# Turning the feed-forward's inner values by DMA, as two 16-bit planes, instead of on TensorE

## The chip, the core and the metric

The kernel runs on one core of one Trainium2 chip. The metric is the device time of one execution in microseconds (us). The engines of a core work side by side, each through its own list of instructions in order: TensorE (PE, matmuls, with its weight loads shown apart as PEld), VectorE (DVE), ScalarE (ACT), GpSimd (POOL) and SyncE (SP, which here only issues DMAs). They wait for one another through semaphores. DMAs that any of them issues run on the core's 16 DMA engines.

## The reference

Two transformer blocks on 256 tokens of width 1024. What is computed between the four feed-forwards (attention of several kinds, gating, pooling) is not touched by the change. A feed-forward is

```
def swiglu(x, w_gate, w_up, w_down):
    return (jax.nn.silu(x @ w_gate) * (x @ w_up)) @ w_down

h = h + FFN_RES * swiglu(rms_norm(h, ffn1_norm[l]), ffn1_w_gate[l], ffn1_w_up[l], ffn1_w_down[l])
```

with 2816 inner values per token. It stands four times in the program: twice in the first block, once in each layer of the second. All is in 32-bit floats.

## The kernel before

**Weights.** All weights stream through SBUF in 404 units of 128 x 1024 values (512 KB). SP loads a unit with two DMAs of 256 KB into one of three buffers `raw`, as soon as VectorE is done with what was there (`free_raw`, line 411, which waits for `low_done`). ScalarE rounds the unit to its high part `wh` (`split`, line 661, the copy at line 659), VectorE takes the difference to get the low part `wl` (`split`, line 1173, the subtraction at line 1182) and then counts up `low_done`. There are six pairs `wh`/`wl`, so both engines may be up to six units ahead of TensorE, which counts up `units_used` when it is done with one. A product in full precision is three matmuls: high by high, high by low, low by high (`products`, lines 1799 to 1801). A unit is 12 matmuls of 512 columns.

**A feed-forward** (`ffn`, once in each engine's program; `f` is 0 to 3) cuts the 2816 inner values into 11 chunks of 256. In the names of TensorE's code, `gate_up(c)` is four units and computes gate and up of chunk c+1 into banks 0 and 1; `down_unit(c, 0)` and `down_unit(c, 1)` multiply chunk c by the down weights. Between them ScalarE computes silu of the gate half (line 721), VectorE multiplies with up (`mul_step`, line 1245) and so writes the inner values `hid`, which lie in the tensor `scores`, with tokens on the partitions. The down product needs them turned. In the kernel before TensorE does that with four 128 x 128 transposes against an identity (`transpose_hidden`, line 1893) into bank 6; ScalarE copies bank 6 rounded to `hTh` (`ht_step`, line 727), VectorE writes `hTl`, the difference (line 1251). `ht_high` and `ht_low` count the two.

**Order around it.** TensorE's loop over c from 1 to 8 is `gate_up(c)`, a wait for `ht_low`, the two down units of c, the transposes of c+1. So the transposes of a chunk run right after the down units of the chunk before, and their result is wanted only after four further units. ScalarE's loop `body` is four splits, silu, two splits, `ht_step`. VectorE's is the same with `mul_step` in the place of silu. Both engines split four units ahead (`LEAD`): while TensorE begins the down units of a chunk, the splits right behind silu are those of the third and fourth unit of the next `gate_up`. Counted from a silu as number 0, with the unit u+8 as the first of the two down units then running, the two splits behind silu are units u+12 and u+13, and the next four are u+14 to u+17. The next `gate_up` is units u+10 to u+13, the down units behind it u+14 and u+15.

**Loads of other kinds.** GpSimd issues bulk loads of its own, of constants and of the second input, while feed-forwards 0 and 1 run.

Of the kernel before, what the change touches and what calls it, by code (L numbers as in the profile page):

```python
# [22 lines left out]
F32 = mybir.dt.float32  # L23
F32R = mybir.dt.float32r
I32 = mybir.dt.int32
ACT = mybir.ActivationFunctionType
AX = mybir.AxisListType

P = 128
T = 256  # L30
NT = T // P
# [3 lines left out]
FC = 256  # L35
NFC = FF // FC
# [92 lines left out]
def two_block_kernel(nc, d, out):  # L129
    ctx = ExitStack()  # L130
    with ctx:
# [3 lines left out]
        def sem(name):  # L135
            return ctx.enter_context(nc.semaphore(name))
# [75 lines left out]
        hid = scores[:, :, 0:FC]  # L212

# [62 lines left out]
        ht_low = sem("ht_low")  # L276
        acc_done = sem("acc_done")
# [371 lines left out]
        def _(act):  # L649
# [66 lines left out]
            def ffn(f, tail=None):  # L716
# [7 lines left out]
                def ht_step(c, dst):  # L724

                    act.wait_ge(ht_psum, NFC * f + c + 1)
                    copy(dst, bank[6][:, :]).then_inc(ht_high, 1)

                def body(c, dst):
                    for i in range(4):  # L730
                        split(u + 4 + i, c)

                    act.wait_ge(units_used, u + 8 + 6 * c)
                    silu_step(c + 1)
                    for i in range(2):
                        split(u + 8 + i, c)
                    ht_step(c + 1, dst)
# [16 lines left out]
                ht_step(0, hTh[:, :, :])  # L754
                with act.Fori(0, NFC - 2, 1) as c:
                    body(c, hTh[:, :, :])

                body(NFC - 2, aTh[:, 6:8, :])
# [402 lines left out]
        def _(dve):  # L1161
# [76 lines left out]
            def ffn(f, done, norm_after, tail=None):  # L1238
# [14 lines left out]
                def body(c, low, high):  # L1253
                    for i in range(4):
                        split(u + 4 + i, c)
                    mul_step(c + 1)
                    for i in range(2):
                        split(u + 8 + i, c)
                    ht_step(c + 1, low, high)
# [5 lines left out]
                with dve.Fori(0, NFC - 2, 1) as c:  # L1265
                    body(c, hTl[:, :, :], hTh[:, :, :])

                body(NFC - 2, aTl[:, 6:8, :], aTh[:, 6:8, :])
# [524 lines left out]
        def _(pe):  # L1793
# [90 lines left out]
            def ffn(f, norm_after, middle=None, late=None):  # L1884
# [40 lines left out]
                transpose_hidden(1)  # L1925
                with pe.Fori(1, NFC - 2, 1) as c:
                    gate_up(c)

                    pe.wait_ge(ht_low, NFC * f + 1 + c)
                    for k in range(2):  # L1930
                        down_unit(c, k)
                    transpose_hidden(c + 1)

                c = NFC - 2
                gate_up(c)
# [553 lines left out]
```

## Time and profile before

| | us |
|---|---|
| median of 3 runs | 1237.26 |
| the runs | 1236.86 to 1239.22 |
| the profiled execution | 1238.18 |
| its span, first to last instruction | 1236.0 |
| TensorE busy | 1226.8 |
| VectorE busy | 750.8 |
| ScalarE busy | 646.2 |

The profiled execution lies 0.9 us over the median, and 2.2 us of it lie around the span. Busy time of TensorE counts the matmuls' modelled durations, which overlap; how fast it goes is read from the distance between the starts of its matmuls. The granted clock of TensorE is 1.000 over the whole span. "Idle" behind a row of a timeline is the time in which the engine stood before that instruction, and what ended it.

### The profile page before, as it was taken

The page shows a single profiled execution, that of the slowest core. Times are in us where ns is not written, and L with a number is a line of the kernel's source. Part 1 is how long each engine was busy: PE and PEld are TensorE (multiplying, and loading weights), DVE is VectorE, ACT ScalarE, POOL GpSimd, SP SyncE. Part 2 cuts the span into 40 slices and gives each one's busy share as a digit, 9 for nine tenths or more (in the row PEclk, how much of TensorE's full clock was granted, in tenths as well). Part 3 has the DMA queues.
Part 4 walks back from the last instruction along what each step waited for, and adds up shares of the span by engine and source line. Part 5 has one row for each costly group of instructions (what it writes and reads, how often), then busy time and mean ns, then how long its engine had stood idle before and what let it go on. Part 6 is the DMA issues. An engine that isn't in the chain of part 4 may idle for free.

```text
span 1236.0 us, 17479 instructions
## 1 busy us (share of the span) xinstructions
PE 1226.8 (99%) x5862; PEld 1009.8 (82%) x5862; DVE 750.8 (61%) x1017; ACT 646.2 (52%) x939; POOL 67.7 (5%) x122
## 2 busy tenths in 40 slices
PE   8999999999999999999999999999999999999998
PEld 7888888877788888888888788888888887888887
DVE  5554546697775564547768666654556666655544
ACT  6454445575555454446666566544445456643442
POOL 0540000000000000000220110000000000000000
PEclk9999999999999999999999999999999999999999
DMA  7876564544555776564555416756565553665662
GB/s 221 238 233 188 186 204 137 179 145 154 161 162 155 247 220 191 184 203 139 177 162 187 154 60 182 231 177 196 181 199 161 163 164 92 199 209 184 189 198 91
DMA packets 166737, 219.43 MB, mean 178 GB/s; under 512 B 13680, under 2 KB 108640, under 8 KB 166560
## 3 DMA queue, kind: packets, MB, share of 16 engines
q1 hardware_dynamic: 164608, 213.70, 55.4%
q0 software_dynamic: 1648, 4.75, 1.3%
q8 instruction: 30, 0.49, 0.2%
q10 hardware_dynamic: 432, 0.33, 0.1%
q14 instruction: 19, 0.16, 0.0%
HBM read 217.68 MB, written 1.05 MB: 177 GB/s over the span
## 4 chain that ended last, share of the span: by engine, by line
PE 96%; ACT 1%; DVE 1%; DMA 1%; issue 0%; SPq 0%; POOL 0%; ACTq 0%; DVEq 0%; POOLq 0%
PE bank L1799 29%; PE bank L1801 29%; PE bank L1800 29%; PE bank L1855 2%; PE bank L1893 2%; PE bank L2051 1%; PE bank L2038 1%; PE bank L2067 1%; PE bank L2036 0%; ACT sb_wh L659 0%; ACT sb_probs L1101 0%; DMA sb_raw<-w_up 0%; PE bank L1972 0%; DVE sb_wl L1182 0%; PE bank L2388 0%
## 5 line engine op out<-in xcount | busy, mean ns | idle before, releaser
L1182 DVE TENSOR_TENSOR sb_wl<-sb_raw,sb_wh 128x1024 fp32r<-128x1024 f32 x403 | 485.2, 1223 | 219.5 <-ACT sb_wh L659 214.6
L659 ACT ACTIVATE sb_wh<-sb_raw 128x1024 fp32r<-128x1024 f32 (+1 forms) x405 | 419.5, 1055 | 231.4 <-DMA sb_raw<-ffn_w_up 74.7
L1799 PE MATMUL bank<-sb_wh,sb_aTh 128*128 128x512 f32 (+1 forms) x1132 | 443.6, 392 | 1.2 <-DVE sb_wl L1182 0.7
L1801 PE MATMUL bank<-sb_wh,sb_aTl 128*128 128x512 f32 (+1 forms) x1132 | 434.9, 384 | 0.0
L1800 PE MATMUL bank<-sb_wl,sb_aTh 128*128 128x512 f32 (+1 forms) x1132 | 434.1, 384 | 0.0
L1801 PEld LDWEIGHTS bank<-sb_wh,sb_aTl 128*128 128x128 f32 x1132 | 212.7, 188 | 43.2
L1799 PEld LDWEIGHTS bank<-sb_wh,sb_aTh 128*128 128x128 f32 x1132 | 212.8, 188 | 42.3 <-issue 2.0
L1800 PEld LDWEIGHTS bank<-sb_wl,sb_aTh 128*128 128x128 f32 x1132 | 213.1, 188 | 39.2
L1799 PE MATMUL bank<-sb_wh,sb_hTh 128*128 128x512 f32 x320 | 124.9, 390 | 0.0
L1801 PE MATMUL bank<-sb_wh,sb_hTl 128*128 128x512 f32 x320 | 124.7, 390 | 0.0
L1800 PE MATMUL bank<-sb_wl,sb_hTh 128*128 128x512 f32 x320 | 124.5, 389 | 0.0
L721 ACT ACTIVATE sb_junk<-bank,sb_rstd 128x256 f32<-128x256 f32 x88 | 36.9, 470 | 100.9 <-PE bank L1801 100.9
L1245 DVE SCALAR_TENSOR_TENSOR sb_scores<-bank,sb_rstd,sb_junk 128x256 f32<-128x256 f32 x88 | 38.5, 479 | 74.3 <-ACT sb_junk L721 74.3
L1799 PE MATMUL bank<-sb_wh,sb_yTh 128*128 128x512 f32 x192 | 77.6, 404 | 0.0
L1801 PE MATMUL bank<-sb_wh,sb_yTl 128*128 128x512 f32 x192 | 75.0, 391 | 0.0
L1800 PE MATMUL bank<-sb_wl,sb_yTh 128*128 128x512 f32 x192 | 74.9, 390 | 0.0
L659 ACT ACTIVATE sb_hTh<-bank 128x512 fp32r<-128x512 f32 x40 | 23.8, 595 | 96.3 <-PE bank L1893 96.3
L1251 DVE TENSOR_TENSOR sb_hTl<-bank,sb_hTh 128x512 fp32r<-128x512 f32 x40 | 27.6, 691 | 70.6 <-ACT sb_hTh L659 70.5
L1801 PEld LDWEIGHTS bank<-sb_wh,sb_hTl 128*128 128x128 f32 x320 | 60.1, 188 | 12.5
L1800 PEld LDWEIGHTS bank<-sb_wl,sb_hTh 128*128 128x128 f32 x320 | 60.1, 188 | 12.4
L1799 PEld LDWEIGHTS bank<-sb_wh,sb_hTh 128*128 128x128 f32 x320 | 60.1, 188 | 12.3
L659 ACT ACTIVATE sb_aTh<-bank,sb_vecs 128x256 fp32r<-128x256 f32 x72 | 28.3, 475 | 38.7 <-PE bank L1855 38.7
(235 smaller groups left out, 835.7 us busy)
## 6 DMA issues: line engine op xcount, KB each, us to landing
sb_raw<-ffn_w_down SPq DMA_DIRECT2D x88, 256.0 KB, 3.0
sb_raw<-w_gate SPq DMA_DIRECT2D x88, 256.0 KB, 3.4
sb_raw<-w_up SPq DMA_DIRECT2D x88, 256.0 KB, 4.1
sb_raw<-w_down SPq DMA_DIRECT2D x88, 256.0 KB, 2.9
sb_raw<-ffn_w_gate SPq DMA_DIRECT2D x87, 256.0 KB, 3.4
sb_raw<-ffn_w_up SPq DMA_DIRECT2D x87, 256.0 KB, 4.2
sb_raw<-w_in SPq DMA_DIRECT2D x80, 256.0 KB, 3.0
sb_raw<-e_w_in SPq DMA_DIRECT2D x40, 256.0 KB, 3.0
```

Source lines behind the costliest of these rows:

```text
L659: return act.activation(dst, src, ACT.Copy, scale=scale)
L721: act.activation(silu[:, t, :], bank[first_bank + t][:, 0:FC], ACT.Silu, scale=rs(norm, t))\
L1182: dve.tensor_tensor(wl[:, u % NSPLIT, :], raw[:, u % NRAW, :], wh[:, u % NSPLIT, :].bitcast(F32), ALU.subtract).then_inc(low_done, 1)
L1245: dve.scalar_tensor_tensor(hid[:, t, :], bank[first_bank + t][:, FC:2 * FC], rs(norm, t), silu[:, t, :], ALU.mult, ALU.mult).then_inc(h_re ...
L1251: dve.tensor_tensor(low, bank[6][:, :], high.bitcast(F32), ALU.subtract).then_inc(ht_low, 1)
L1799: pe.matmul(dst, lh, w_hi, start=start, stop=False)
L1800: pe.matmul(dst, lh, w_lo, start=False, stop=False)
L1801: return pe.matmul(dst, ll, w_hi, start=False, stop=stop)
L1855: ins = pe.transpose(dst[:, T * j + P * t:T * j + P * t + P], tiles(j, t), ident[:])
L1893: ins = pe.transpose(bank[6][:, T * j + P * t:T * j + P * t + P], hid[:, t, tok(j)], ident[:])
L2038: pe.matmul(bank[4 + i % 2][:, P:3 * P], q[:, P:T], k[:, 0:T], start=True, stop=True).then_inc(at.s_psum, 1)
L2051: ins = pe.transpose(bank[6][:, tok(j)], probs[:, i % 4, tok(j)], ident[:])
```

## The change

The inner values of chunks 1 to 9 of each feed-forward are turned by a DMA. Chunks 0 and 10 keep TensorE's transposes. A DMA transpose takes 16-bit elements, so the 32-bit values are split into a plane of the lower and a plane of the upper halves, turned as bits, and joined again.

- ScalarE, behind silu and one split, waits for `mul_step` (`h_ready`), copies the lower and the upper halves of `hid` into `planes` (two copies of 128 x 512 values of 16 bits, read at a step of two), does the next split, whose instruction also waits for `planes_done`, and issues one DMA transpose of `planes` into `planesT` (256 KB, eight blocks of 128 x 128).
- VectorE, in the next pass of the loop and behind three of its four splits, waits for the DMA (`planes_turned`) and joins the halves in `hT` with two copies of 128 x 512 (`join_step`). After the fourth split it waits for `ht_high` and writes `hTl` (`turned_step`), and only then comes to `mul_step`.
- ScalarE, behind its four splits and ahead of silu, waits for `hT_joined` and copies `hT`, rounded, to `hTh`.
- TensorE loses the transposes of chunks 1 to 9, 36 groups of four in the program. In their place it waits for `h_ready` ahead of `gate_up`, since `gate_up` overwrites the banks from which `mul_step` reads.

```
 [ScalarE]
-                def ht_step(c, dst):
+                def ht_step(n, dst):

-                    act.wait_ge(ht_psum, NFC * f + c + 1)
+                    act.wait_ge(ht_psum, 2 * f + n)
                     copy(dst, bank[6][:, :]).then_inc(ht_high, 1)

-                def body(c, dst):
+                def planes_step(c):
+
+                    act.wait_ge(h_ready, 2 * NFC * f + 2 + 2 * c)
+                    for h in range(2):
+                        ins = copy(planes.rearrange("p (h t c) -> p h t c", h=2, t=NT)[:, h], hid_halves[:, h])
+                    ins.then_inc(planes_done, 1)
+
+                def turned_step(c):
+
+                    act.wait_ge(hT_joined, (NFC - 2) * f + c)
+                    copy(hTh[:, :, :], hT).then_inc(ht_high, 1)
+
+                def turn_hidden():
+                    act.dma_start_transpose(planesT.rearrange("p (b r) -> p b r", r=P), planes).then_inc(planes_turned, 16)
+
+                def body(c, turned, tail_chunk=False):
                     for i in range(4):
                         split(u + 4 + i, c)
+                    if turned:
+                        turned_step(c)

                     act.wait_ge(units_used, u + 8 + 6 * c)
                     silu_step(c + 1)
-                    for i in range(2):
-                        split(u + 8 + i, c)
-                    ht_step(c + 1, dst)
+                    split(u + 8, c)
+                    if tail_chunk:
+                        split(u + 9, c)
+                        return
+                    planes_step(c + 1)
+
+                    act.wait_ge(planes_done, (NFC - 2) * f + 1 + c)
+                    split(u + 9, c)
+                    turn_hidden()
 [VectorE]
+                def join_step(c):
+
+                    dve.wait_ge(planes_turned, 16 * (NFC - 2) * f + 16 * c)
+                    turned = planesT.rearrange("p (h t k r) -> p h k t r", h=2, t=NT, k=2)
+                    for h in range(2):
+                        ins = dve.tensor_copy(hT_halves[:, h], turned[:, h])
+                    ins.then_inc(hT_joined, 1)
+
+                def turned_step(c):
+
+                    dve.wait_ge(ht_high, NFC * f + c + 1)
+                    dve.tensor_tensor(hTl[:, :, :], hT, hTh[:, :, :].bitcast(F32), ALU.subtract).then_inc(ht_low, 1)
+
-                def body(c, low, high):
-                    for i in range(4):
+                def body(c, turned):
+                    for i in range(3):
                         split(u + 4 + i, c)
+                    if turned:
+                        join_step(c)
+                    split(u + 7, c)
+                    if turned:
+                        turned_step(c)
                     mul_step(c + 1)
                     for i in range(2):
                         split(u + 8 + i, c)
-                    ht_step(c + 1, low, high)
 [TensorE]
-                transpose_hidden(1)
                 with pe.Fori(1, NFC - 2, 1) as c:
+
+                    pe.wait_ge(h_ready, 2 * NFC * f + 2 + 2 * c)
                     gate_up(c)

                     pe.wait_ge(ht_low, NFC * f + 1 + c)
                     for k in range(2):
                         down_unit(c, k)
-                    transpose_hidden(c + 1)
```

The lists of instructions show what moved. ScalarE's loop, from silu to the loop's end, before (`sb_junk` holds silu):

```order
L721 ACTIVATE sb_junk<-bank,sb_rstd 128x256 [waits units_used]
L721 ACTIVATE sb_junk<-bank,sb_rstd 128x256
L669 REGISTER_ALU
L672 REGISTER_ALU [waits loaded0]
L659 ACTIVATE sb_wh<-sb_raw 128x1024 [waits units_used]
L659 ACTIVATE sb_wh<-sb_raw 128x1024 [waits units_used,loaded1]
L726 REGISTER_ALU
L659 ACTIVATE sb_hTh<-bank 128x512 [waits ht_psum]
L755 REGISTER_ALU
L755 COMPARE_AND_BRANCH
```

and in the changed kernel, from the copy to `hTh` on (`sb_probs` holds both planes and turned planes, `sb_probsT` is `hT`):

```order
L668 ACTIVATE sb_hTh<-sb_probsT 128x512 [waits hT_joined]
L759 REGISTER_ALU
L730 ACTIVATE sb_junk<-bank,sb_rstd 128x256 [waits units_used]
L730 ACTIVATE sb_junk<-bank,sb_rstd 128x256
L678 REGISTER_ALU
L681 REGISTER_ALU [waits loaded0]
L668 ACTIVATE sb_wh<-sb_raw 128x1024 [waits units_used]
L740 ISA
L668 ACTIVATE sb_probs<-sb_scores 128x512 [waits h_ready]
L668 ACTIVATE sb_probs<-sb_scores 128x512
L668 ACTIVATE sb_wh<-sb_raw 128x1024 [waits units_used,loaded1,planes_done]
L751 DMA_TRANSPOSE sb_probs<-sb_probs 128x8x128
```

The copy to `hTh` went from behind the second split to a place ahead of silu, and two copies stand between the two splits, with the DMA behind them. VectorE's loop, from the third of its four splits on, before:

```order
L1182 TENSOR_TENSOR sb_wl<-sb_raw,sb_wh 128x1024 [waits high_done]
L1181 REGISTER_ALU
L1182 TENSOR_TENSOR sb_wl<-sb_raw,sb_wh 128x1024 [waits high_done]
L1244 ISA
L1245 SCALAR_TENSOR_TENSOR sb_scores<-bank,sb_rstd,sb_junk 128x256 [waits silu_done]
```

and in the changed kernel:

```order
L1216 TENSOR_TENSOR sb_wl<-sb_raw,sb_wh 128x1024 [waits high_done]
L1289 REGISTER_ALU
L1292 COPY sb_probsT<-sb_probs 128x512 [waits planes_turned]
L1292 COPY sb_probsT<-sb_probs 128x512
L1215 REGISTER_ALU
L1216 TENSOR_TENSOR sb_wl<-sb_raw,sb_wh 128x1024 [waits high_done]
L1297 REGISTER_ALU
L1298 TENSOR_TENSOR sb_hTl<-sb_probsT,sb_hTh 128x512 [waits ht_high]
L1278 ISA
L1279 SCALAR_TENSOR_TENSOR sb_scores<-bank,sb_rstd,sb_junk 128x256 [waits silu_done]
```

The two copies that join and the subtraction to `hTl` now stand around the fourth split, behind the third, where the subtraction came before only after two further splits.

## Rows read from the trace of the kernel before

**Rows 1.** The page: engines' busy time, and the chain that ended last.

```profile
PE 1226.8 (99%) x5862; PEld 1009.8 (82%) x5862; DVE 750.8 (61%) x1017; ACT 646.2 (52%) x939; POOL 67.7 (5%) x122
PE 96%; ACT 1%; DVE 1%; DMA 1%; issue 0%; SPq 0%; POOL 0%; ACTq 0%; DVEq 0%; POOLq 0%
```

**Rows 2.** TensorE's waits, the largest in total: us in total, times, longest.

```profile
PE bank L2377 <- DVE sb_probs L1708: 2.1, 4, 0.8
```

**Rows 3.** Timeline of TensorE, one chunk: start us, us, instruction.

```profile
105.38 0.39 PE L1801 MATMUL bank<-sb_wh,sb_hTl 128*128 128x512 f32 x1
105.61 0.60 PE L1893 MATMUL bank<-sb_ident,sb_scores 128*128 128x128 f32 x4
...
108.12 0.39 PE L1799 MATMUL bank<-sb_wh,sb_aTh 128*128 128x512 f32 x1
...
116.96 0.39 PE L1799 MATMUL bank<-sb_wh,sb_hTh 128*128 128x512 f32 x1
```

**Rows 4.** Timeline of ScalarE, same chunk; "x2" are two instructions.

```profile
100.36 0.84 ACT L721 ACTIVATE sb_junk<-bank,sb_rstd 128x256 f32<-128x256 f32 x2 [3.36 <-PE bank L1801]
101.09 2.01 ACT L659 ACTIVATE sb_wh<-sb_raw 128x1024 fp32r<-128x1024 f32 x2
...
106.73 2.00 ACT L659 ACTIVATE sb_wh<-sb_raw 128x1024 fp32r<-128x1024 f32 x2
110.01 1.06 ACT L659 ACTIVATE sb_wh<-sb_raw 128x1024 fp32r<-128x1024 f32 x1 [1.27 <-DMA sb_raw<-ffn_w_up]
```

**Rows 5.** Timeline of VectorE, same chunk.

```profile
102.18 2.36 DVE L1182 TENSOR_TENSOR sb_wl<-sb_raw,sb_wh 128x1024 fp32r<-128x1024 f32 x2 [0.44 <-ACT sb_wh L659]
...
111.10 1.23 DVE L1182 TENSOR_TENSOR sb_wl<-sb_raw,sb_wh 128x1024 fp32r<-128x1024 f32 x1 [0.92 <-ACT sb_wh L659]
113.90 1.22 DVE L1182 TENSOR_TENSOR sb_wl<-sb_raw,sb_wh 128x1024 fp32r<-128x1024 f32 x1 [1.58 <-ACT sb_wh L659]
```

**Rows 6.** Timeline of SP, same chunk: the load of unit u+16 begins.

```profile
104.98 0.38 SPq L440 DMA_DIRECT2D sb_raw<-ffn_w_gate  x1
```

**Rows 7.** Groups by line: busy us, mean ns of one.

```profile
L659 ACT ACTIVATE sb_wh<-sb_raw 128x512 fp32r<-128x512 f32 x2 | 1.1, 628 | 0.0
L1708 DVE TENSOR_SCALAR sb_probs<-sb_probs,sb_rinv 128x256 f32<-128x256 f32 x16 | 4.9, 351 | 0.3
L1492 DVE COPY sb_gates<-bank 128x512 f32<-128x512 f32 x2 | 1.4, 687 | 2.3 <-PE bank L1855 2.3
L1251 DVE TENSOR_TENSOR sb_hTl<-bank,sb_hTh 128x512 fp32r<-128x512 f32 x40 | 27.6, 691 | 70.6 <-ACT sb_hTh L659 70.5
```

**Rows 8.** The page: DMA queue (packets, MB, share), and an issue's us to landing.

```profile
q1 hardware_dynamic: 164608, 213.70, 55.4%
sb_raw<-ffn_w_up SPq DMA_DIRECT2D x87, 256.0 KB, 4.2
```

**Rows 9.** Stretches: us, each engine's busy time, clock, DMA share, GB/s.

```profile
62.00:64.00 2.00, 2.00 (x10) 1.66 (x9) 0.00 (x0) 0.00 (x0) 1.44 (x7) 1.00 1.06 349
102.50:104.50 2.00, 2.00 (x11) 1.65 (x10) 2.00 (x2) 0.60 (x1) 0.00 (x0) 1.00 0.00 0
```

**Rows 10.** Timelines in feed-forwards 0 and 1: VectorE, ScalarE and TensorE beside GpSimd's bulk loads.

```profile
64.75 1.06 ACT L659 ACTIVATE sb_wh<-sb_raw 128x1024 fp32r<-128x1024 f32 x1 [7.38 <-DMA sb_raw<-ffn_w_down]
66.56 0.39 PE L1799 MATMUL bank<-sb_wh,sb_hTh 128*128 128x512 f32 x1
436.70 0.39 PE L1799 MATMUL bank<-sb_wh,sb_hTh 128*128 128x512 f32 x1
437.57 2.54 DVE L1182 TENSOR_TENSOR sb_wl<-sb_raw,sb_wh 128x1024 fp32r<-128x1024 f32 x2 [2.00 <-ACT sb_wh L659]
```

**Rows 11.** Timelines at feed-forward 2's first pass: ScalarE, VectorE, TensorE.

```profile
775.62 0.82 ACT L721 ACTIVATE sb_junk<-bank,sb_rstd 128x256 f32<-128x256 f32 x2
787.46 1.23 DVE L1182 TENSOR_TENSOR sb_wl<-sb_raw,sb_wh 128x1024 fp32r<-128x1024 f32 x1 [1.50 <-ACT sb_wh L659]
790.16 0.39 PE L1799 MATMUL bank<-sb_wh,sb_hTh 128*128 128x512 f32 x1
```

More of the change, by code:

```diff
@@ L25 @@
 I32 = mybir.dt.int32
+U16 = mybir.dt.uint16
 ACT = mybir.ActivationFunctionType
@@ L212, in two_block_kernel @@
         hid = scores[:, :, 0:FC]
+        hid_halves = scores[:, :, :].bitcast(U16).rearrange("p t (c h) -> p h t c", h=2)[:, :, :, 0:FC]
+        planes = probs[:, 2, :].bitcast(U16)
+        planesT = probs[:, 3, :].bitcast(U16)
+        hT = probsT[:, 0, :].rearrange("p (k t) -> p k t", k=2)
+        hT_halves = probsT[:, 0, :].bitcast(U16).rearrange("p (k t r h) -> p h k t r", k=2, t=NT, h=2)
         soft = shared[:, 0:768].rearrange("p (s c) -> p s c", s=2)
@@ L276, in two_block_kernel @@
         ht_low = sem("ht_low")
+        planes_done = sem("planes_done")
+        planes_turned = sem("planes_turned")
+        hT_joined = sem("hT_joined")
         acc_done = sem("acc_done")
@@ L753, in ffn @@
                 splits(u + 2, 2)
[L754 to L758, printed above, removed]
+                ht_step(1, hTh[:, :, :])
+                body(0, False)
+                with act.Fori(1, NFC - 2, 1) as c:
+                    body(c, True)
+                body(NFC - 2, True, True)
+                ht_step(2, aTh[:, 6:8, :])
                 if tail is not None:
@@ L1264, in ffn @@
                 ht_step(0, hTl[:, :, :], hTh[:, :, :])
-                with dve.Fori(0, NFC - 2, 1) as c:
-                    body(c, hTl[:, :, :], hTh[:, :, :])
-                body(NFC - 2, aTl[:, 6:8, :], aTh[:, 6:8, :])
+                body(0, False)
+                with dve.Fori(1, NFC - 2, 1) as c:
+                    body(c, True)
+                body(NFC - 2, True)
+                ht_step(NFC - 1, aTl[:, 6:8, :], aTh[:, 6:8, :])
                 if tail is not None:
@@ L1931, in ffn @@
                         down_unit(c, k)
-                    transpose_hidden(c + 1)
                 c = NFC - 2
+                pe.wait_ge(h_ready, 2 * NFC * f + 2 + 2 * c)
                 gate_up(c)
```

## The prediction

> **What bounds the kernel now.** I read the page first. TensorE is busy for 99% of the span and the chain that ended last is TensorE for 96% of it [rows 1]. The list of waits confirms it: the wait that costs TensorE most in the whole program sums to 2.1 us [rows 2]. So the time is the number of matmuls by their distance, and two things alone move it: work taken from TensorE, and a wait of TensorE that was not there. Busy times of ScalarE and VectorE (52% and 61%) say that there is room on average. Whether there is room at the right moment is what the timelines are for. In a steady chunk ScalarE stands idle for 3.36 us ahead of silu, until TensorE ends the four gate and up units [rows 4]; the splits behind silu are therefore tied to TensorE's pace, and their loads after them.
>
> **What the change removes.** The matmul ahead of the four transposes starts at 105.38 and the tenth behind them at 108.12, 2.74 us [rows 3]. From there the next down unit, 39 matmuls on, starts at 116.96: 8.84 / 39 = 0.2267 us each. Ten steps would be 2.27 us, so a group of transposes costs 0.47 us. 36 groups go: 36 x 0.47 = 16.9 us, all on the path, since TensorE never waits there. ScalarE's and VectorE's old steps for the turned values (0.69 us on VectorE [rows 7]) are replaced by others of the same kind.
>
> **What it adds, in a steady chunk.** The new chain is: silu, product, two plane copies, DMA, join, copy to hTh, subtraction to hTl; it must end before the next down unit. What matters is not its own length but what it queues behind and what queues behind it.
>
> (a) Plane copies. 128 x 512 from SBUF on ScalarE took 0.63 us [rows 7]; two of them, with the overlap of 0.1 us that two splits in a row show (2.01 us for 2 x 1.06) [rows 4], are 1.05 us. They stand ahead of the split of unit u+13. VectorE was done with that unit at 102.18 + 2.36 = 104.54 [rows 5], and is now at 105.6. The load of u+16, which needs this buffer, began at 104.98 [rows 6], and begins 0.6 us later.
>
> (b) The DMA. No row shows a transpose. Its 0.26 MB at the rate that the weight queue shows while it is busy, 213.7 MB / (0.554 x 1236 us) = 312 GB/s [rows 8], take 0.85 us of all DMA engines. If it is cut into 1,024 rows of 128 values, each as dear as that queue's mean packet, 0.554 x 16 x 1236 / 164,608 = 67 ns [rows 8], it takes 1,024 x 67 / 16 = 4.3 us. I take 1.1 us, near the lower end, since these rows carry a fifth of that mean packet's bytes. The DMA engines have idle stretches (0 GB/s from 102.5 to 104.5 us [rows 9]), but not there: it is issued at about 103.1 + 1.05 = 104.2, when u+15 and u+16 are being loaded. Of 0.6 us of (a) and 1.1 us of (b) I put 0.7 us on the arrival of u+16, because a load that begins later stands less long behind that of u+15. So VectorE ends u+16 at 111.10 + 1.23 + 0.7 = 113.0 [rows 5]. The planes themselves, landed after 4.2 us like a weight load of that size [rows 8], are there at 108.4, 4.6 us early. How long ScalarE is held by the issue is not shown either. SP's 0.38 us [rows 6] is the nearest row; ScalarE's next splits, u+14 and u+15, began at 106.73 before [rows 4], so an issue of up to 2.5 us from 104.2 on delays nothing.
>
> (c) The join. It stands behind the split of u+16. A copy of 128 x 512 took 0.69 us from PSUM, an operation of 128 x 256 within SBUF 0.35 us [rows 7]; the copies lie between 0.35 and 0.69. I take 0.45, so 0.9 us for both: 113.9.
>
> (d) The split of u+17 on VectorE, 1.15 us, and the subtraction, 0.69 us less 0.1 of overlap [rows 5, 7]: 115.7. ScalarE's copy to hTh (0.63 us) runs beside the split.
>
> (e) The deadline is the next down unit: 116.96 - 0.47 = 116.5. The chain is 0.8 us early. At the low ends (nothing for the DMA, 0.35 us a copy) it is 1.7 us early. At the high ends (4.3 us and 0.69 us) it is nearly 4 us late. What hid the old chain was 9 us of air between the transposes and their use; now there is under one.
>
> How lateness is paid: silu waits for the gate and up units, not for the down units that stall. So if the chain is x late, the next chunk's chain starts as early as ever and its deadline lies x later. A chain that is y late in every chunk then costs y/2 a chunk.
>
> **Where the deadline is missed in any case.** In a feed-forward's first pass the splits run behind. In feed-forward 2 silu starts at 775.62, though TensorE had ended the units before it one chunk (72 x 0.2267 + 0.47 = 16.8 us) ahead of 790.16, at 773.4 [rows 11]. VectorE ends u+16 at 787.46 + 1.23 = 788.7. With the same 0.7 + 0.9 + 1.15 + 0.6 = 3.35 us the chain ends at 792.0; the deadline is 790.16 - 0.47 = 789.7: 2.3 us of stall. Feed-forwards 1 and 3 read alike, 0 is just in time: 3 x 2.3 = 6.9 us.
>
> GpSimd's bulk loads collide twice with the stream. From 62 to 64 us the DMA engines are full at 349 GB/s [rows 9], ScalarE waits 7.38 us and splits u+16 only from 64.75 [rows 10]. TensorE did not notice, since it had split units in store. Now the join stands behind that split: 64.75 + 1.06 + 1.23 + 3.35 = 70.4 against a deadline of 66.56 - 2 x 0.47 = 65.6: 4.8 us. In feed-forward 1: 437.57 + 1.23 + 3.35 = 442.15 against 436.70 - 0.94 + 2.3 (the stall before it) = 438.1 [rows 10]: 4.1 us. Together 8.9 us.
>
> The clock: every row shows a granted clock of 1.00, full speed, and TensorE's longest wait among those costliest is 0.8 us [rows 2, 9]. The Trainium skill (TensorE: Matmul & The Clock Gate, Rules for kernel authors) warns that idle gaps between bursts of matmuls of the length of the largest stalls here can take the clock to its lower level. No row here shows that, and the sum holds nothing for it; it would add to the slower side.
>
> **Sum.** -16.9 + 6.9 + 8.9 = -1.1 us. The profiled execution's 1238.18 becomes 1237.1; that execution lies 0.9 us over the median, so I forecast **1236 us**. A measurement of this kernel can tell about 0.2% (2.5 us) from no change, so this is no change: the work saved is given back as five stalls.
>
> **Rivals.**
>
> *The chain is cheap.* The stream has air, so the DMA delays nothing, the copies take 0.35 us (0.9 us less in the chain), and the first passes catch up because the old steps no longer stand among their splits. Then only the collisions remain, 4.8 + 4.1 less 0.9 each and with the stall of 2.3 gone from the second one's deadline: 3.9 + 5.5 = 9.4, at most; at the least, if the second collision's chain also catches up, 7. Net some -8.5 us: 1229. For it: the DMA engines' share of 0.55. Against: they are full just where it counts.
>
> *Late in every chunk: slower.* The transpose's packets cost DMA time above (b), u+16 comes later, the join with it. It decides from 0.8 us above my sum; at 1.8 us above, the chain is 1 us late, 31 chunks by 0.5 us and 5 stalls by 1 us: +20 us, 1257. For it: the interval of (b) reaches 3.2 us above my value. Against: the rate at which wide packets move, and idle stretches ahead of the loads.
>
> *The transpose itself is long.* It may take 8.8 us before the join waits for it (113.0 - 104.2). If its eight blocks go one after another and it lands after 12.6 us, three times a load's 4.2, the chain ends at 104.2 + 12.6 + 0.9 + 1.15 + 0.6 = 119.5, 3 us late: 31 x 1.5 = 46 us more in the chunks and up to 3 us at each of the five stalls, some 1290. Against it: a load of the same size lands after 4.2 us [rows 8]. The Trainium skill (VectorE: DVE Perf Modes, The three transpose paths) gives 1309 ns for one 128 x 128 block by DMA; eight in a row would be 10.5 us, an estimate from that page, which the trace of before can neither confirm nor deny, and by which the chain would be 0.9 us late.
>
> **Chances.** Forecast case 0.42 (1231 to 1243), cheap chain 0.20, late in every chunk 0.31, long transpose 0.07. Faster by over 0.2% (under 1234.8): 0.20 and four tenths of the first, 0.37. Slower (over 1239.7): 0.29 + 0.07 and a seventh of the first, 0.42. Within: 0.21. Range 1226 to 1262: it reaches from a little below the cheap chain's time to a little above that of the late chain, and leaves out the long transpose and the edges.
>
> **What would show it.** Distance of TensorE's starts at the end of a down unit back to 0.2267 us with no 1893 group: the gain. In TensorE's waits, VectorE's subtraction to hTl as releaser: about five waits, of 2 to 5 us, at the first passes of feed-forwards 1 to 3 and near 66 and 438 us. About 35 such waits: the late chain. VectorE's join waiting for the DMA and not for the split ahead: the long transpose. Plane copies other than 0.6 us, join copies other than 0.45 us, and u+16 later by other than 0.7 us would correct a term each. The forecast is wrong if the first passes or the collisions do not stall TensorE, or if the steady chunks do.

## The result, and the profile after

The changed kernel took **1244.35 us** (median of 7 runs, 1240.77 to 1249.9) against 1237.32 for the kernel before beside it (7 runs, 1236.86 to 1239.22): ratio **1.0055**, 95% interval 1.0045 to 1.0064. It is 7 us slower; the forecast was 1236 us, no change. The profiled execution took 1245.88 us, with a span of 1244.1, 8.1 us longer than before. The runs spread more than those of before, 9 us against 2.4.

The page of the changed kernel: the DMA queue that carries the transposes (packets, MB, share of 16 engines), and the chain that ended last.

```profile
q10 hardware_dynamic: 38448, 9.77, 4.6%
PE 81%; DMA 7%; DVE 4%; ACT 4%; issue 2%; SPq 1%; ACTq 0%; POOL 0%; DVEq 0%; POOLq 0%
```

TensorE's share of the chain fell from 96% [rows 1] to 81%: DMA, VectorE and ScalarE now stand in it, a sign of stalls. It is no measure of them: 15% of the span are 187 us, and the stalls are 19, since behind each stall the chain is followed back over the other engines for much longer than TensorE stood. TensorE's waits, the two largest (us in total, times, longest):

```profile
PE bank L1852 <- DVE sb_hTl L1298: 17.9, 6, 4.8
PE bank L2432 <- DVE sb_probs L1761: 2.1, 4, 0.8
```

The second row is what was the largest before [rows 2]. The first is new: six waits for VectorE's subtraction to hTl. By the starts of the matmuls around them, less a normal step of 0.227 us, their lengths are 2.55 and 4.99 us (feed-forward 0, at 49 and 68 us), 1.25 and 3.72 (feed-forward 1, at 424 and 442), 3.55 (feed-forward 2, at 797) and 2.87 (feed-forward 3, at 1094): 18.9 us in all. All are in chunk 1 or 2. The one in feed-forward 2, in TensorE's timeline:

```profile
797.24 0.39 PE L1854 MATMUL bank<-sb_wh,sb_aTl 128*128 128x512 f32 x1
801.02 0.79 PE L1852 MATMUL bank<-sb_wh,sb_hTh 128*128 128x512 f32 x1 [3.39 <-DVE sb_hTl L1298]
801.61 0.63 PE L1853 MATMUL bank<-sb_wl,sb_hTh 128*128 128x512 f32 x1
802.03 0.63 PE L1854 MATMUL bank<-sb_wh,sb_hTl 128*128 128x512 f32 x1
```

Behind the stall a matmul takes 0.63 us where it took 0.39 before it, and the starts lie 0.43 us apart, not 0.227. Stretches around the longest stall show why (stretch; us; busy time of TensorE, its weight loads, VectorE, ScalarE and GpSimd; granted clock; DMA share; GB/s):

```profile
68.00:70.00 2.00, 0.06 (x1) 0.00 (x0) 0.92 (x1) 1.60 (x2) 1.66 (x5) 1.00 0.52 145
70.00:72.00 2.00, 0.00 (x0) 0.00 (x0) 2.00 (x4) 1.44 (x4) 1.83 (x3) 0.55 0.55 167
72.89:76.30 3.41, 3.41 (x8) 2.76 (x9) 2.23 (x4) 2.69 (x4) 2.59 (x7) 0.50 0.67 230
80.00:84.00 4.00, 4.00 (x19) 3.31 (x18) 0.95 (x2) 1.42 (x2) 0.00 (x0) 1.00 1.02 282
```

The granted clock fell to 0.50, the lower of the two levels (1.2 GHz), while TensorE stood, and stayed there for the first 4 us of work. This came at four of the six stalls, those of 4.99, 3.72, 3.55 and 2.87 us; the half-speed stretches are 6.8 us (part of it inside the stall) and three times 3.4 us long. In the kernel before, the clock was at 1.00 throughout.

In the steady chunks TensorE does not wait, as forecast. One of them: VectorE from the split of u+15 on, ScalarE's copies and the issue of the DMA, and TensorE's first matmul of the down units:

```profile
116.76 1.23 DVE L1216 TENSOR_TENSOR sb_wl<-sb_raw,sb_wh 128x1024 fp32r<-128x1024 f32 x1 [2.05 <-ACT sb_wh L668]
118.48 1.23 DVE L1216 TENSOR_TENSOR sb_wl<-sb_raw,sb_wh 128x1024 fp32r<-128x1024 f32 x1 [0.50 <-ACT sb_wh L668]
119.62 0.80 DVE L1292 COPY sb_probsT<-sb_probs 128x512 uint16<-128x512 uint16 x2
121.22 1.23 DVE L1216 TENSOR_TENSOR sb_wl<-sb_raw,sb_wh 128x1024 fp32r<-128x1024 f32 x1 [0.80 <-ACT sb_wh L668]
122.36 0.69 DVE L1298 TENSOR_TENSOR sb_hTl<-sb_probsT,sb_hTh 128x512 fp32r<-128x512 f32 x1
...
109.46 1.14 ACT L668 ACTIVATE sb_probs<-sb_scores 128x512 uint16<-128x512 uint16 x2
...
110.64 1.25 ACTq L751 DMA_TRANSPOSE sb_probs<-sb_probs  x1
...
123.91 0.39 PE L1852 MATMUL bank<-sb_wh,sb_hTh 128*128 128x512 f32 x1
```

The chain ends at 123.05, 0.9 us ahead of the matmul that needs it (0.8 to 1.9 us in the 26 steady chunks of the trace, 1.3 at the median); the join waits for the split ahead of it and not for the DMA.

### The profile page after: what moved, and what is told of

It is laid out like the page before. It is cut to its first block, busy times and chain, and to the rows that moved or that the text cites. A ratio compares the mean times of both kernels' runs of the same rounds, so it can differ in the third digit from the quotient of the medians.

```text
span 1244.1 us, 17351 instructions
## 1 busy us (share of the span) xinstructions
PE 1216.9 (98%) x5718; PEld 999.6 (80%) x5718; DVE 776.9 (62%) x1089; ACT 692.0 (56%) x1011; POOL 66.6 (5%) x122
## 4 chain that ended last, share of the span: by engine, by line
PE 81%; DMA 7%; DVE 4%; ACT 4%; issue 2%; SPq 1%; ACTq 0%; POOL 0%; DVEq 0%; POOLq 0%
PE bank L1852 25%; PE bank L1854 25%; PE bank L1853 25%; DMA sb_raw<-ffn_w_up 4%; ACT sb_wh L668 2%; DVE sb_wl L1216 2%; PE bank L1908 2%; DMA sb_raw<-w_up 2%; PE bank L2106 1%; SPq L449 1%; PE bank L2093 1%; DMA sb_raw<-w_out 1%; PE bank L2122 1%; PE bank L2091 0%; ACT sb_probs L1135 0%
## 5 line engine op out<-in xcount | busy, mean ns | idle before, releaser
L668 ACT ACTIVATE sb_wh<-sb_raw 128x1024 fp32r<-128x1024 f32 (+1 forms) x405 | 425.6, 1057 | 283.0 <-DMA sb_raw<-ffn_w_down 50.5
L1852 PE MATMUL bank<-sb_wh,sb_hTh 128*128 128x512 f32 x320 | 128.5, 402 | 17.9 <-DVE sb_hTl L1298 17.9
L1853 PEld LDWEIGHTS bank<-sb_wl,sb_hTh 128*128 128x128 f32 x320 | 61.9, 193 | 12.9
L1229 DVE SCALAR_TENSOR_TENSOR sb_aTl<-bank,sb_vecs,sb_aTh 128x256 fp32r<-128x256 f32 x72 | 30.0, 477 | 25.5 <-ACT sb_aTh L668 25.3
L1854 PEld LDWEIGHTS bank<-sb_wh,sb_yTl 128*128 128x128 f32 x192 | 36.0, 188 | 7.8
```

The lines of the kernel that those rows point to most:

```text
L668: return act.activation(dst, src, ACT.Copy, scale=scale)
L1229: dve.scalar_tensor_tensor(aTl[:, k, :], bank[6 + g % 2][:, T * j:T * j + T], vecs[:, col + k:col + k + 1], aTh[:, k, :].bitcast(F32), ALU ...
L1852: pe.matmul(dst, lh, w_hi, start=start, stop=False)
L1853: pe.matmul(dst, lh, w_lo, start=False, stop=False)
L1854: return pe.matmul(dst, ll, w_hi, start=False, stop=stop)
```

## The experiments

All ratios are against the kernel before, run beside them (medians 1237.6 to 1237.9). A helper number: with no stall and the clock at 1.00, a feed-forward takes 155.5 us from the transposes of chunk 0 to those of chunk 10 (159.9 before), so the 36 groups are worth 4 x 4.36 = 17.4 us. The first rows below are the changed kernel's feed-forward 1, the last two the same place in the kernel with an early join and loads apart (below):

```profile
402.27 0.60 PE L1946 MATMUL bank<-sb_ident,sb_scores 128*128 128x128 f32 x4
564.51 0.60 PE L1946 MATMUL bank<-sb_ident,sb_scores 128*128 128x128 f32 x4
```

```profile
392.91 0.60 PE L1967 MATMUL bank<-sb_ident,sb_scores 128*128 128x128 f32 x4
548.43 0.60 PE L1967 MATMUL bank<-sb_ident,sb_scores 128*128 128x128 f32 x4
```

162.24 less 155.52 is 6.7 us, of which the two stalls are 4.97; the other 1.75 us are lost in the matmuls behind the stalls. The same in feed-forward 0 gives 9.75 - 7.54 = 2.2 us, in 2 and 3 together 9.74 - 6.42 = 3.3 us: 7.3 us in all. Not all of it is the clock's: behind the two stalls that left the clock at 1.00, 60 steps also took 0.14 us more than 60 x 0.2267. Six times 0.14 taken off, **6.4 us of clock** are left, 1.4 to 1.9 us for each of the four falls. The balance of the four feed-forwards is -17.4 + 18.9 + 7.3 = +8.8 us; the rest of the program was 0.7 us shorter, which gives the +8.1 of span.

### 1. The join earlier

```diff
 [ScalarE]
-for i in range(4): split(u + 4 + i, c)
-if turned: turned_step(c)
+for i in range(2): split(u + 4 + i, c)
+if turned: turned_step(c)
+for i in range(2, 4): split(u + 4 + i, c)
 [VectorE]
-for i in range(3): split(u + 4 + i, c)
-if turned: join_step(c)
-split(u + 7, c)
-if turned: turned_step(c)
+split(u + 4, c)
+if turned: join_step(c)
+split(u + 5, c)
+if turned: turned_step(c)
+for i in range(2, 4): split(u + 4 + i, c)
```

> The changed kernel with the chain taken forward: VectorE joins behind the first of its four splits (not the third) and subtracts behind the second; ScalarE copies to hTh behind its second split. Everything is still computed. Theory A (the stalls come from the join's place behind the split of unit u+16, and the clock's fall comes from the stalls): the join now stands behind u+14, which is split some 4 us earlier even where the stream is late, so the six waits of TensorE for hTl (18.9 us over a normal step in the changed kernel) go but for at most one or two, the granted clock stays at 1.00, and what is left is the gain of 36 groups of transposes, 16.9 us: about 1237.3 - 16.9 = 1220 us, 1219 to 1224. Rival B (the transpose lands late, or the added DMA traffic delays the stream itself): the join waits for the DMA, issued some 4 us before, or the splits come late anyway; four or more of the six stalls stay, and the time stays over 1236 us.

1227.28 us (5 runs, 1226.36 to 1230.96), ratio 0.9923, interval 0.991 to 0.9937. TensorE's wait for hTl:

```profile
PE bank L1855 <- DVE sb_hTl L1300: 4.0, 2, 3.4
```

Theory A in its mechanism, but 7 us over the 1220 us that it named and 3 over its band: four of six stalls went; those left are 0.7 and 3.6 us long, and the clock fell once. The larger one, at 66 us, has a new cause: the DMA transpose is itself late, and the join waits for it:

```profile
66.93 0.81 DVE L1294 COPY sb_probsT<-sb_probs 128x512 uint16<-128x512 uint16 x2 [1.69 <-DMA sb_probs<-sb_probs]
```

It stands behind a split of ScalarE that came at 60.03 us (54.25 in the changed kernel), beside GpSimd's loads, and landed 6.9 us after its issue, where the median is 4.4.

### 2. The join between the two places

The same edit with the join behind the second split, the subtraction and ScalarE's copy behind the third.

> The place between the two: join behind VectorE's second split (unit u+15), subtraction behind the third; ScalarE's copy to hTh behind its third. Theory (each stall shrinks by the time between VectorE's splits of u+15 and u+16 at its place in the changed kernel's trace: 1.5 of 2.55 us, 2.7 of 4.99, 1.7 of 1.25, 1.5 of 3.72, 3.6 of 3.55, about as much in feed-forward 3): three stalls stay, 1.1 + 2.3 + 2.2 us, with at most one fall of the clock: 1237.6 - 16.9 + 5.6 + 0 to 1.5 = 1226 to 1228 us. Rival (the stalls come from the DMA transpose's own landing or from a stream slowed everywhere, not from the order on VectorE): little difference from the changed kernel, 1240 us or more.

1232.23 us (4 runs), ratio 0.996, interval 0.9946 to 0.9975. The profiled execution took 1231.4 us:

```profile
PE bank L1854 <- DVE sb_hTl L1299: 8.6, 5, 5.0
```

Most of the effect is there and the order of the three places is as the theory has it (1244, 1232, 1227 us), but it is 4 us over the sum. Stall by stall the theory did less well. In feed-forward 0 the first was 1.2 us for 1.1 and the second, at 66 us, 5.2 for 2.3, with the one long fall of the clock behind it; in feed-forward 1 the second was 1.2 for 2.2; in feed-forward 2, where none was expected, 1.4.

### 3. Without the DMA

```diff
-                    turn_hidden()
...
-                    dve.wait_ge(planes_turned, 16 * (NFC - 2) * f + 16 * c)
-                    turned = planesT.rearrange(...)
+                    dve.wait_ge(planes_done, (NFC - 2) * f + c)
+                    turned = planes.rearrange(...)
```

> The changed kernel without its 36 DMA transposes: VectorE joins the planes as they lie, so the inner values of chunks 1 to 9 are not turned (this part of the computation is left out). ScalarE no longer spends its 1.25 us a chunk on the issue, and 9.4 MB less go through the DMA engines. Every copy, split and wait keeps its place. Theory A (place): the stalls stay, only shorter by what the DMA added to the arrival of unit u+16, 0.7 us each in the prediction: six stalls of some 2 to 4.5 us, about 1244.3 - 6 x 0.7 - 2 for a clock that falls less often = 1238 us. Rival B (the DMA or its issue makes the stalls): most of them go, and the time falls to 1220 to 1226 us.

1237.31 us (10 runs), ratio 0.9999, interval 0.999 to 1.0009.

```profile
PE bank L1851 <- DVE sb_hTl L1297: 12.0, 6, 3.4
```

All six stalls stay, 12.9 us in all instead of 18.9, with two falls of the clock instead of four. Five are 1.1 to 1.5 us shorter, the first of feed-forward 1 is 0.6 us longer (1.9 us). So the stalls are there without the DMA, as the theory of the place has it; the DMA and its issue add 1.0 us to each on average, by one trace of each kernel.

### 4. All that was added, nothing removed

TensorE keeps its transposes; plane copies, DMA transposes and joins are done beside them, into a tensor that nobody reads.

> The kernel before, with all that the change adds and nothing of what it removes: plane copies, the 36 DMA transposes issued from ScalarE at the same place, and VectorE's two join copies behind its third split, into a tensor that nobody reads. TensorE keeps its transposes, and what it waits for is the old chain. Theory A (what costs is only that TensorE's input now stands behind u+16): TensorE does not wait, and the time is that of before, 1237 us, within 2 us. Rival B (the added work or traffic itself pushes the splits beyond their deadlines): TensorE waits for wl or wh at the two collisions or in the first passes, and the time is 1241 us or more.

1239.73 us (10 runs, 1236.76 to 1245.79), ratio 1.002, interval 1.0006 to 1.0034: at the upper end of what theory A allows. The profiled execution, 1241.7 us, shows where the 2 us come from:

```profile
PE bank L1840 <- DVE sb_wl L1211: 2.9, 2, 2.1
```

TensorE waits at 69 us for a split: with the added work GpSimd's loads empty the store of split units, which they did not do before. This wait is 2.3 us long, the clock fell behind it, and the 60 matmuls behind it took 1.4 us more than normal: 3.7 of the 3.9 us of span over the kernel before. Elsewhere in this trace the added work is free.

### 5. TensorE turns chunks 1 and 2 too

```diff
-                with pe.Fori(1, NFC - 2, 1) as c:
+                for c in (1, 2):
+                    transpose_hidden(c)
+                    gate_up(c)
+                    pe.wait_ge(ht_low, NFC * f + 1 + c)
+                    for k in range(2):
+                        down_unit(c, k)
+                with pe.Fori(3, NFC - 2, 1) as c:
```

> The changed kernel with chunks 1 and 2 of each feed-forward turned by TensorE as before, and only chunks 3 to 9 by DMA. Eight groups of transposes come back, 8 x 0.47 = 3.8 us. Theory A: the six stalls are all in the first or second chunk turned by DMA while the stream of weights is behind; from chunk 3 on it has caught up. The stalls go, the clock stays at 1.00, and 28 x 0.47 = 13.2 us are gained: 1237.3 - 13.2 = 1224 us, 1222 to 1227. Rival B (whichever chunk is the first turned by DMA meets the stall, since the chain's own length makes it): four stalls stay at chunk 3, and the time is 1234 us or more.

1232.92 us (10 runs, 1226.74 to 1235.79), ratio 0.9959, interval 0.9945 to 0.9973. That is over theory A's band; the profiled execution, 1229.11 us, was one of two in which the clock stayed at 1.00. In feed-forwards 2 and 3 theory A held, no stall is left. In 0 and 1 chunk 3 stalls now (TensorE's timeline at 85 and 453 us):

```profile
85.05 0.49 PE L1874 MATMUL bank<-sb_wh,sb_hTh 128*128 128x512 f32 x1 [2.60 <-DVE sb_hTl L1310]
453.52 0.49 PE L1874 MATMUL bank<-sb_wh,sb_hTh 128*128 128x512 f32 x1 [2.41 <-DVE sb_hTl L1310]
```

These are 2.76 and 2.57 us by the starts. They could have been read from the trace of the kernel before: there VectorE ended u+16 of chunk 3 only 0.8 us (at 82.05) and 1.8 us (at 451.25) ahead of the deadline of (e), where a steady chunk has 4 to 5 us. The stream needs longer than one chunk to recover from GpSimd's loads.

### 6. GpSimd's loads apart

GpSimd's bulk loads of these two feed-forwards in pieces of at most 256 KB, one or two of them behind each wait for `units_used` from the 30th unit of the feed-forward on; one of them as example:

```diff
-pool.dma_start(gates[:, 0, :], bass.AP(bg.tensor, bg.offset, [[0, P], [1, 2 * D]])).then_inc(bias_in, 16)
+for i in range(4):
+    pool.wait_ge(units_used, 30 + 3 * i)
+    w = 2 * D // 4
+    pool.dma_start(gates[:, 0, i * w:(i + 1) * w], bass.AP(bg.tensor, bg.offset + i * w, [[0, P], [1, w]])).then_inc(bias_in, 16)
```

> The changed kernel with GpSimd's bulk loads of feed-forwards 0 and 1 cut in pieces of at most 384 KB and issued later, one each three to six units, instead of all at once near 53 to 57 us and 425 to 430 us. The chain keeps its place. Theory A (two of the six stalls, those of 4.99 and 3.72 us, come from these loads that push back the weight stream): both go, with the two stretches at half speed behind them that came after 73 and 446 us (6.8 and 3.4 us long, some 4.5 us of loss), and the other four stay: 1244.3 - 8.7 - 4.5 = 1231 us, 1229 to 1235. Rival B (the second chunk is late because it follows the first pass, whatever GpSimd loads): both stalls stay, 1242 us or more.

1236.3 us (10 runs, 1233.04 to 1238.97), ratio 0.999, interval 0.998 to 0.9999.

```profile
PE bank L1870 <- DVE sb_hTl L1316: 9.6, 5, 2.9
```

The stalls at 68 and 442 us are gone, as theory A has it: these two came from the loads. One of 1.5 us came at 517 us, behind a later piece, the clock fell behind those at 49 and 787 us (for 3.4 and 6.8 us), and the time is 1 us over the expected band.

### 7. The stalls filled

```diff
+FILL = ((7, 16), (0, 12), (11, 0), (9, 0))
...
+                    for _ in range(FILL[f][c - 1]):
+                        pe.matmul(bank[6][:, :], aTh[:, 0, tok(0)], aTh[:, 0:2, :], start=True, stop=True)
                     pe.wait_ge(ht_low, NFC * f + 1 + c)
```

> The changed kernel with filler for TensorE ahead of its wait for hTl: matmuls of 128x512 on values that lie there anyway, into bank 6, which nobody reads at that time; 7 and 16 of them in chunks 1 and 2 of feed-forward 0, 12 in chunk 2 of feed-forward 1, 11 and 9 in chunk 1 of feed-forwards 2 and 3, each set about 1 us shorter than the stall it fills (stalls of 2.55, 4.99, 3.72, 3.55 and 2.87 us, a matmul 0.227 us). The input of the down units comes as late as before, so nothing of the stalls is gained; but TensorE never stands for long. Theory A (what is left unexplained, about 6 us, is the clock's fall after the stalls): the granted clock stays at 1.00, no stretch of 3.4 us at half speed, and the time falls by 5 to 7 us to 1237 to 1239 us. Rival B (the clock falls for another reason, or its cost is not these 6 us): 1244 us or more, since filler never shortens the chain.

Median 1248.37 us (6 runs, 1238.95 to 1257.13), ratio 1.0108, interval 1.0083 to 1.0132. The profiled execution was the 1238.95 one: clock at 1.00 throughout, and 7 us less than the changed kernel's, as theory A has it. The input was about as late as there, 18.2 us over the six places for 18.9. The other five had clocks of 0.992 to 0.997 and no trace, and the median lies 4 us above the changed kernel's, where rival B would put it. A second trace of the same kernel:

> The same kernel as the one with filled stalls, for a second trace: its profiled execution had a granted clock of 1.00 and 1239.0 us, but its others had 0.992 to 0.997 and up to 1257 us. Reading A (the stream's timing differs from one execution to the next, and a stall longer than its filler plus 2.5 us lets the clock fall all the same, and a filler then runs at half speed in the next chunk): this trace, if it is a slow one, shows stalls behind the fillers of over 2.5 us or stalls where no filler stands, each with a stretch at 0.5. Reading B (the filler itself takes the clock down): stretches at 0.5 that begin inside or right behind fillers with no stall ahead of them.

1250.86 us in its profiled execution, 1253.16 median of 2. TensorE at feed-forward 0, chunk 2, where the filler ends and the wait begins:

```profile
68.14 3.79 PE L1984 MATMUL bank<-sb_aTh 128*128 128x512 f32 x16
77.58 0.79 PE L1853 MATMUL bank<-sb_wh,sb_hTh 128*128 128x512 f32 x1 [5.65 <-DVE sb_hTl L1299]
```

Here the input was 4.4 us later than in the changed kernel's trace, and TensorE stood for 5.65 us behind the filler; in feed-forward 1, chunk 1, which had no filler, for 4.54 us. The clock fell at both, and no fall came inside or behind a filler without a stall. Reading A. Why the input is later in most executions of this kernel is not shown. The trace also shows that the size of the stalls differs from one execution to the next: ScalarE got unit u+15 at 65.30 us in the changed kernel's trace and at 70.14 here, behind the same loads.

### 8. Pauses of known length

```diff
 [GpSimd]
+for c in range(1, 9):
+    pool.wait_ge(units_used, FIRST["ffn3"] + 8 + 6 * c)
+    pool.memset(qkT[...][:, 0:PAUSE[c - 1]], 0.0).then_inc(pause_over, 1)
 [TensorE]
                     gate_up(c)
+                    if f == 3:
+                        pe.wait_ge(pause_over, c)
                     pe.wait_ge(ht_low, NFC * f + 1 + c)
```

> The kernel before, with eight pauses of TensorE of rising length in feed-forward 3, one in each of chunks 1 to 8, 17 us or more apart: ahead of its wait for hTl TensorE waits for GpSimd to clear 1100, 1600, 2100, 2400, 2700, 3000, 3500 and 4096 values per partition, about 1 ns each. It measures the disputed price by itself. Theory A (a stall of about 3 us or more takes the granted clock to 0.5 for 3.4 us after it, which costs half of that, 1.7 us; shorter stalls cost their own length): the pauses of 1.1 to 2.4 us leave the clock at 1.00, those from about 2.8 us on do not; three or four falls: pauses of 20.5 us and some 0.3 us of overhead each, 23 us, plus 5 to 7 us: 1237.5 + 29 = 1266 us. Rival B (the clock falls for another reason, such as the DMA traffic or the changed kernel's own work): no falls, 1260 us. Rival C (any stall over 1 us can do it): falls after the short ones too, 1270 us or more.

1267.07 us (4 runs), 1263.0 in the profiled one, span 1260.8. The pauses by the starts of the matmuls were 1.29, 1.71, 2.12, 2.37, 2.62, 2.87, 3.29 and 3.79 us, 20.1 in all. TensorE behind the fourth, the fifth and the seventh, and stretches behind these and the eighth:

```profile
1144.62 0.40 PE L1806 MATMUL bank<-sb_wl,sb_hTh 128*128 128x512 f32 x1
...
1163.83 0.50 PE L1805 MATMUL bank<-sb_wh,sb_hTh 128*128 128x512 f32 x1 [2.46 <-POOL sb_qkT L649]
1164.17 0.56 PE L1806 MATMUL bank<-sb_wl,sb_hTh 128*128 128x512 f32 x1
1164.53 0.63 PE L1807 MATMUL bank<-sb_wh,sb_hTl 128*128 128x512 f32 x1
...
1206.84 0.50 PE L1805 MATMUL bank<-sb_wh,sb_hTh 128*128 128x512 f32 x1 [3.13 <-POOL sb_qkT L649]
1207.17 0.40 PE L1806 MATMUL bank<-sb_wl,sb_hTh 128*128 128x512 f32 x1
```

```profile
1145.70:1149.00 3.30, 3.30 (x17) 2.71 (x16) 0.58 (x1) 0.00 (x0) 0.00 (x0) 1.00 0.66 206
1164.40:1167.40 3.00, 3.00 (x8) 2.33 (x8) 1.18 (x2) 0.00 (x0) 0.00 (x0) 0.50 0.50 177
1208.00:1211.00 3.00, 3.00 (x15) 2.47 (x14) 0.00 (x0) 0.00 (x0) 0.00 (x0) 1.00 0.77 254
1229.10:1231.90 2.80, 2.80 (x8) 2.23 (x7) 0.00 (x0) 0.00 (x0) 0.00 (x0) 0.50 0.84 281
```

Theory A, but without the bound that it put near 2.8 us: the clock fell after 2.62, 2.87 and 3.79 us and did not after 3.29. In the other traces it fell after stalls of 2.0 us (loads apart, at 51 us) and 2.3 us (all added, at 69 us), and not after 2.56, 2.75 (chunks 1 and 2 on TensorE) and 2.91 us (loads apart). Each of the seven stalls over 3.3 us in the traces without filler was followed by a fall. The price: from one group of transposes to the next (16.80 us without a pause) the five chunks without a fall are longer than their pause by 0.14 to 0.16 us, the three with one by 1.75, 1.49 and 1.75: **1.3 to 1.6 us a fall** of 3.4 us at half speed. In the other traces falls of that length cost 1.3 to 1.6 us too, and those of 6.8 us 1.9 to 2.9. GpSimd's clearing stands for any stall here: no DMA transpose runs in this kernel, so the falls belong to the standing, not to the change's own work. The other three runs had clocks of 0.992 instead of 0.996, about twice the time at half speed, and 4 to 5 us more.

### 9. Early join and loads apart

> Both together: the join behind the first split, as in the run with the early join (1227.3 us, with stalls of 0.7 and 3.6 us left, both in feed-forward 0, the larger at the bulk loads and followed by a stretch at half speed), and GpSimd's loads in pieces and later. Theory: the stall of 3.6 us and its 1.5 us of clock go: 1227.3 - 5.1 = 1222 us, 1220.5 to 1223.5, the whole gain of 36 x 0.47 us but for 1 to 2 us. Rival (what is left in the early-join kernel over 1220.7 us has other causes, such as wider spread of the DMA traffic): 1225 us or more.

**1220.57 us** (4 runs, 1219.86 to 1220.97), ratio **0.9859**, interval 0.9845 to 0.9873: 17.3 us faster than before, 24 us faster than the change as made. TensorE's largest wait and the page's DMA queue of the transposes are

```profile
PE bank L2453 <- DVE sb_probs L1782: 2.1, 4, 0.8
q10 hardware_dynamic: 38448, 9.77, 4.9%
```

and the steady chunk on VectorE (join, split, subtraction) with the matmul that needs it:

```profile
107.13 0.80 DVE L1312 COPY sb_probsT<-sb_probs 128x512 uint16<-128x512 uint16 x2 [2.40 <-DMA sb_probs<-sb_probs]
109.03 1.23 DVE L1236 TENSOR_TENSOR sb_wl<-sb_raw,sb_wh 128x1024 fp32r<-128x1024 f32 x1 [1.10 <-ACT sb_wh L686]
110.17 0.68 DVE L1318 TENSOR_TENSOR sb_hTl<-sb_probsT,sb_hTh 128x512 fp32r<-128x512 f32 x1
...
113.91 0.39 PE L1873 MATMUL bank<-sb_wh,sb_hTh 128*128 128x512 f32 x1
```

The same DMAs run, the join now waits for them, and the chain still ends 3 us early in this chunk, where the one shown of the changed kernel was 0.9 early; the least in the trace is 0.5 us. The spread of the runs is 1.1 us. Both edits are needed: the early join alone gave 1227, the loads apart alone 1236.

## Why the prediction was wrong

**The step that failed is the clock**, the paragraph whose "sum holds nothing for it". The forecast had stalls of 4.8 and 4.1 us in its own sum and gave them no price but their length. The trace of before could not show the price, since its clock never fell. The Trainium skill (TensorE: Matmul & The Clock Gate, Why this matters for your kernels; the prediction gives the section another name), cited there as a warning, pointed the right way: the clock fell at four of the six stalls. Four falls cost 6.4 us in the profiled execution, and pauses of known length gave 1.3 to 1.6 us each. Of the 9.9 us by which the four feed-forwards missed the sum (+8.8 for -1.1), 7.3 stand behind the stalls, 6.4 of them the clock's, and 3.1 are longer stalls; the gain was 0.5 us better.

The seven runs fit this: their mean clocks were 0.992 to 0.995. Each 0.001 below 1 is 2.5 us of 1244 at half speed, at most 1.24 us lost; taken off, the seven times are 1233 to 1240 us, median 1237. This takes off somewhat too much, 8.7 us for the profiled execution, where the starts of the matmuls give 6.4, since part of the half speed lies inside the stalls. What is left lies in the band of the forecast case.

**The gain** was right: 16.9 us forecast, 17.4 measured.

**The first passes** were undersized: none, 2.3, 2.3, 2.3 us forecast, 2.55, 1.25, 3.55 and 2.87 measured, 10.2 for 6.9. Most of the miss is a reading. Feed-forward 0 was called "just in time", but in the trace of before it stands like the others. VectorE's split of its u+16, and the down unit that sets the deadline:

```profile
47.02 1.23 DVE L1182 TENSOR_TENSOR sb_wl<-sb_raw,sb_wh 128x1024 fp32r<-128x1024 f32 x1 [1.01 <-ACT sb_wh L659]
49.74 0.39 PE L1799 MATMUL bank<-sb_wh,sb_hTh 128*128 128x512 f32 x1
```

47.02 + 1.23 + 3.35 = 51.6 against 49.74 - 0.47 = 49.3 is 2.3 us of stall. The same working for feed-forwards 1 and 3 gives 2.0 and 2.6, so 9.2 us for the four. The rest is the 0.7 us put on the arrival of u+16: against its deadline it came 1.0, 0.0, 2.0 and 0.2 us later than before.

**The collisions** were right in place and cause, and gone with the loads apart; that the sizes came so close, 4.8 and 4.1 us forecast, 4.99 and 3.72 measured, is in part luck. The first starts from the wrong unit: ScalarE's split at 64.75 loads from `ffn_w_down` [rows 10], so it is u+15, the second down unit. u+16 is the next:

```profile
66.49 1.06 ACT L659 ACTIVATE sb_wh<-sb_raw 128x1024 fp32r<-128x1024 f32 x1 [0.68 <-DMA sb_raw<-ffn_w_up]
67.59 2.57 DVE L1182 TENSOR_TENSOR sb_wl<-sb_raw,sb_wh 128x1024 fp32r<-128x1024 f32 x2 [0.52 <-ACT sb_wh L659]
```

67.59 + 1.23 + 3.35 = 72.2, against a deadline of 65.6 + 2.3 for the stall before it, is 4.2 us: the wrong unit and the missing stall cancel. With both readings put right, and the second collision's deadline moved by 2.0 us instead of 2.3, the sum is -16.9 + 9.2 + 4.2 + 4.4 = +0.9 us instead of -1.1: 1238 us, and still no change; what was left to miss was the clock. What was not foreseen either is that the collisions differ from one execution to the next by 4 us and more.

**The terms of the chain** were mostly good. Plane copies and joins (busy us, mean ns), and the DMA's median us from issue to landing:

```profile
L668 ACT ACTIVATE sb_probs<-sb_scores 128x512 uint16<-128x512 uint16 x72 | 41.2, 623 | 1.1 <-DVE sb_scores L1279 1.1
L1292 DVE COPY sb_probsT<-sb_probs 128x512 uint16<-128x512 uint16 x72 | 28.7, 454 | 0.0
sb_probs<-sb_probs ACTq DMA_TRANSPOSE x36, 4.4
```

623 ns for 0.63, 454 for 0.45, 4.4 us for 4.2. The DMA takes 4.6% of 1244 us over 36, 1.6 us of all engines, for 1.1. Its issue holds ScalarE for 1.25 us, inside the 2.5 us that were free. The 0.7 us on the arrival of u+16 did not come in the steady chunks: in the one shown it is split at 119.71, 4.2 us ahead of the deadline, as before (112.33 against 116.49), and over all steady chunks it is 0.3 us later at the median. Instead the split of u+17 waits for its own load, 0.80 us in the chunk shown. The steady chain is 0.8 to 1.9 us early, for 0.8.

**The rivals.** The cheap chain did not come, because the first passes did not catch up. Late in every chunk did not come: not one steady chunk stalls. The long transpose did not come either; the estimate of 10.5 us from the Trainium skill's figure (VectorE: DVE Perf Modes, The three transpose paths) does not hold for one DMA of eight blocks: here it landed after 4.4 us at the median. The measurement fell inside the range and on the slower side, for which the clock had been named, but the most likely case had left it out.

What stays open: which stall between 2.0 and 3.3 us takes the clock down, why the stream behind GpSimd's loads is 5 us later in one execution than in another, and how much of the first passes' lateness is ScalarE's plane copies, which no run takes out alone.

## What to carry to other kernels

Where TensorE bounds a kernel, price a stall at its length plus what the clock takes after it: here 1.3 to 1.6 us for most falls and up to 2.9 for the longest, at some of the stalls of 2.0 to 3.3 us and at all that were longer. A chain with 9 us of air that is rebuilt with 1 us is late wherever the weight stream is late, so place the new consumer behind the earliest work that it can stand behind, not where its average slack is positive. And when a margin is used up, look for rare bulk loads that the margin had been hiding, and read every such place unit by unit, since a load's name tells which unit it is. Cutting these loads up was worth 8 us with the join late and 7 us with it early.

## What the runs showed of the hardware

- The granted clock fell to 0.50 for 3.4 us after a stall of 2.62 us and stayed at 1.00 after one of 3.29 us in the same execution; it fell during the stall where this was 5 us long. A fall of 3.4 us cost 1.3 to 1.6 us.
- Behind a stall that left the clock at 1.00, 60 matmuls of 128x512 took 0.12 to 0.17 us more than 60 normal steps of 0.2267 us.
- Stalls filled with matmuls left the clock at 1.00 in one execution (1238.95 us); it fell where the lateness outran the filler by 5.65 us.
- A DMA transpose of 128 x 1024 values of 16 bits landed after 4.4 us at the median, but after 13.9 us when issued at 54.3 us among GpSimd's loads, and after 18.3 us at the same place in the second trace of the filled kernel. It took 1.6 us of all 16 DMA engines, and ScalarE 1.25 us to issue.
